# A two-layer hybrid decoder: queries of two expert heads made block by block, half a gate made later, the second block's expert rows written out

## The chip, the cores and the metric

One core of a Trainium2 chip runs the kernel in one launch. The metric is the device time of one execution in microseconds (us). Before the change it is 1875.85 us, the median of three runs (1875.61 to 1876.41).

## The reference

The input is 256 tokens of width 1024, and there are two layers. Each layer has a token mixer (three branches, of which none is touched here, merged by gates and multiplied by an output matrix), a layer norm, and a channel mixer, which is the part that the change is about:

```python
q = (h @ w_q).reshape(B, S, 8, 2, 128)              # 8 heads, two sides each
s1 = einsum('bshd,hnd->bshn', q[..., 0, :], sub_k1)  # 128 scores per side
s2 = einsum('bshd,hnd->bshn', q[..., 1, :], sub_k2)
v1, i1 = top_k(s1, 16); v2, i2 = top_k(s2, 16)       # best 16 of each side
# the best 16 of the 256 sums v1 + v2 name 16 of 128*128 experts
wts = softmax(top_s)
act = gelu(einsum('thkd,td->thk', u_tab[idx], x))    # one dot per expert
out = einsum('thkd->td', act * wts * v_tab[idx])     # weighted sum of rows
ple = sigmoid(h @ ple_gate) * (p @ ple_proj)         # embedding gate, projection
h = layer_norm(alpha * h + out + ple)
```

So every token reads 8 x 16 = 128 expert rows of 2 x 1024 floats (a `u` row and a `v` row, kept side by side, 8 KB), chosen by its own scores.

## The kernel before, in words

The tokens stand in two blocks of 128, one token on each partition. In each layer a dense stage makes the token mixer. Its large products are three fp32r products each (a value split into a high and a low part, lines 760 to 762). Then come the experts, first of block 0, then of block 1.

**A row of experts.** For each of the 128 ranks (8 heads x 16) of a block, GpSimd issues an indirect DMA (line 680 for block 0, line 703 and after it 713 for block 1) that gathers one expert row for each of the 128 tokens, 1 MB, into one of 8 slots. VectorE forms the dot of the `u` half with the tokens (lines 1737, 1767). ScalarE takes gelu, multiplies by the softmax weight and writes a diagonal matrix of the result (lines 1330 to 1334 for block 0, 1354 to 1360 for block 1). TensorE multiplies that diagonal with the `v` half and adds into two PSUM banks `acc` (lines 931, 950). The semaphore `row_used` then frees the slot, and GpSimd may issue the gather of 8 rows later into it. Each fp32 product with 512 columns appears as two records, so that a row is four records of TensorE.

**What else runs beside the rows of block 0.** The order is written out by hand in `steps()`, and all engines follow the same list. Beside a row `("row", r, i)` (number 16r + i) stand steps of TensorE: `wqh` and `wq` (line 791) make the two sides of a head's queries for both blocks at once, 8 products of 256 columns each; `sc` (line 1191) makes a block's 256 scores of a head; `pp` (line 1197) is the embedding's projection; `pgw` (line 823) is a quarter of one half of the embedding gate, for both blocks, four products of 512 columns. Head 0 has its own step per block, `wq0` (line 784), 16 products of 128 columns. Queries of heads 1 and 2 are made ahead of, or in, the first rows; heads 3 to 7 stand beside rows up to 61, `pp` at 62 and 65, the gate from 70 to 106. VectorE picks the 16 best of the head two ahead (`select_head`) in pieces between the dots.

**Block 1** runs in hardware loops: seven turns of a head on GpSimd and TensorE, six on VectorE and ScalarE, with waits against a register and `nop(nofuse=True)` beside them; GpSimd copies eight indices at a time to `stage` (line 695), VectorE copies the scores of a head (line 1552), ScalarE the weights of a head (line 1348). No query, score or gate is left for it.

**Between the blocks** VectorE waits until the last row of block 0 has been added, adds `acc` to block 0's base in two instructions (line 1720) and only then forms block 1's first dot. TensorE waits for that sum, puts block 1's base into `acc` by two products with the identity (line 943) and goes on with the rows.

**The start.** TensorE runs ten products with the identity that nobody reads (`keep_busy`, line 740) before the first transposes of the input (line 836), and ten more after them. Then it makes the pooling branch's input in eight pieces (`poolw`, four quarters of two blocks), with a small product `smallT` between the second and the third quarter, which waits for GpSimd's low part of its weights.

**Weights** come in pieces of 512 KB that SyncE loads through a ring of 7 buffers; some pieces, those of the queries among them, have homes of their own (`EXTRAS`, `extra_home`). A buffer is loaded again once the piece in it has been read (`used`).

Of the kernel before, what the change touches and what calls it, by code (L numbers as in the profile page):

```python
# [25 lines left out]
U32 = mybir.dt.uint32  # L26
ALU = mybir.AluOpType
# [54 lines left out]
SELECT_LINKS = 27  # L82
HALF = TOPK // 2
ROW_LINKS = TOPK


def steps():
# [60 lines left out]
    beside = {(0, 1): [("sc", 0, 2), ("sc", 1, 2)], (0, 6): [("wqh", 1, 1)], (0, 9): [("wq", 1, 1)], (0, 11): [("sc", 0, 3), ("sc", 1, 3)]}  # L148
    halves_at, gate_at = (20, 25, 31, 36, 42, 47, 53, 58), (70, 75, 80, 85, 91, 96, 101, 106)
    beside |= {divmod(n, TOPK): [("wq" if i % 2 else "wqh", 2 + i // 4, i // 2 % 2)] for i, n in enumerate(halves_at)}  # L150
    beside |= {divmod(n + 3, TOPK): [("sc", 0, 4 + i), ("sc", 1, 4 + i)] for i, n in enumerate(halves_at[1::2])}
    beside |= {divmod(62 + 3 * b, TOPK): [("pp", 0, b), ("pp", 1, b)] for b in range(2)}
    beside |= {divmod(n, TOPK): [("pgw", j // 4, j % 4)] for j, n in enumerate(gate_at)}
    beside |= {divmod(gate_at[4 * c + 3] + 1, TOPK): [("pg", c, 0), ("pg", c, 1)] for c in range(2)}
    for r in range(EH):
        for i in range(TOPK):
            s += [("row", r, i)] + beside.get((r, i), [])
    s += [("ln2", 0), ("experts", 1), ("ln2", 1)]
# [3 lines left out]
NO_BANK = {"outa", "wide", "wide_out", "late", "o", "shares", "exps", "softplus", "onorm", "stats", "ln1", "ln2", "select", "texp", "wqh", "pgw", "row", "experts"}  # L162
# [3 lines left out]
def rows_later(kinds, rows):  # L166
# [3 lines left out]
    for step in STEPS[first:]:  # L170
        if step[0] in kinds:
            held.append([rows, step])
            continue
        out.append(step)
        if step[0] == "row":
# [9 lines left out]
def first_products(L):  # L185
# [16 lines left out]
ACT_STEPS = rows_later(("wq", "sc", "pp", "pg"), 1)  # L202
DVE_STEPS = rows_later(("pg",), 2)
FILLS = [s for s in STEPS if s[0] not in NO_BANK]
NBANK = 6


def group_list():
# [20 lines left out]
    for hd in range(EH):  # L229
        if hd:  # L230
            made = ("wq", hd // 2, hd % 2)
            g.append(([made], False, [made, made]))
# [5 lines left out]
    for c in range(2):  # L238
        g.append(([("pg", c, 0), ("pg", c, 1)], False, [None, None, None, ("pg", c, 1)]))
# [7 lines left out]
QUERY_PIECES = [[(GROUP_OF[("wq", hd // 2, hd % 2) if hd else ("wq0", 0)], j) for j in range(2)] for hd in range(EH)]  # L247
KEY_PIECES = [(GROUP_OF["sc", 0, 1], j) for j in range(2)]
PROJECTION_PIECES = [(GROUP_OF["pp", 0, 0], j) for j in range(2)]
EXTRAS = QUERY_PIECES[4] + QUERY_PIECES[5] + PROJECTION_PIECES  # L250
EXTRAS += QUERY_PIECES[3] + QUERY_PIECES[6] + QUERY_PIECES[7] + QUERY_PIECES[1] + QUERY_PIECES[2] + QUERY_PIECES[0] + KEY_PIECES
# [27 lines left out]
def build(nc, x, weights, params, lnrows, consts, experts, cum_rows, out):  # L279
    with ExitStack() as ctx:  # L280
# [88 lines left out]
        stage = sb("stage", 16, U32)  # L369
        upper_lower = sb("upper_lower", 2 * HALVED, U32)  # L370
        wts = sb("wts", NB * RANKS)
        wst, dots, gel, gw = sb("wst", 16), sb("dots", 16), sb("gel", 16), sb("gw", 16)
# [79 lines left out]
        idx_staged, wts_staged = sem("idx_staged"), sem("wts_staged")  # L452
# [47 lines left out]
        def extra_home(L, piece):  # L500
# [6 lines left out]
            if piece in QUERY_PIECES[3]:  # L507
# [83 lines left out]
        def _(sp):  # L591
# [7 lines left out]
            early = QUERY_PIECES[2] + QUERY_PIECES[1] + QUERY_PIECES[3]  # L599
            ahead = {g1 + 2 + 2 * i: early[i:i + 1] for i in range(6)} | {b1 + 8 + 2 * i: QUERY_PIECES[7][i:i + 1] for i in range(2)}  # L600
            ahead |= {o + 2 * i + 1: QUERY_PIECES[6][i:i + 1] for i in range(2)} | {o + 7: QUERY_PIECES[0]}
            ahead |= {o + 10: QUERY_PIECES[4][:1], o + 11: QUERY_PIECES[4][1:], o + 12: QUERY_PIECES[5][:1]}
# [28 lines left out]
        def _(pool):  # L631
# [4 lines left out]
            for L in range(DEPTH):  # L636
                for step in STEPS:
# [45 lines left out]
                    if kind == "experts":  # L683
                        b = step[1]
                        n0 = (L * NB + b) * RANKS

                        def number(r, i):

                            pool.wait_ge(row_used, r * TOPK + (n0 + i + 1))
                            pool.nop(nofuse=True)  # L690
                            if i % HALF == 0:
                                pool.wait_ge(idx_ready, r * 2 + (2 * (L * NB + b) * EH + i // HALF + 1))
                                pool.nop(nofuse=True)
                            if i % RING == 0:
                                nc.gpsimd.tensor_copy(stage[:, i:i + RING], idxu[:, bass.ds(r * TOPK + (b * RANKS + i), RING)]).then_inc(idx_staged, 1)
                                pool.wait_ge(idx_staged, r * 2 + (L * 2 * EH + i // RING + 1))
                                pool.nop(nofuse=True)
                            return bass.IndirectOffsetOnAxis(stage[:, i:i + 1], 0)

                        with pool.Fori(0, EH - 1) as r:  # L700
                            for i in range(TOPK):
                                at_row = number(r, i)
                                nc.gpsimd.indirect_dma_start(slots[i % RING][:, :], None, experts[:, :], at_row).then_inc(slot_in[i % RING], 16)  # L703
                        halves = experts.rearrange("e (s d) -> (e s) d", s=2)
                        for i in range(TOPK):
                            at_row = number(EH - 1, i)
                            if i == RING:
# [1381 lines left out]
```

## Time and profile before

| | |
|---|---|
| median of 3 runs | 1875.85 us |
| the profiled execution: its own time | 1876.75 us |
| its span, first to last instruction | 1874.8 us |
| mean granted clock of TensorE | 0.991 |
| TensorE, VectorE, ScalarE, GpSimd busy | 91%, 73%, 48%, 38% |
| expert gathers (software queue) | 546.57 MB in 75952 packets |
| weights and the like (hardware queue) | 112.74 MB |

Read the shares of busy time as means over two dense stages (about 0 to 289 us and 937 to 1218 us) and two expert stages. The page cuts the span in 40 slices: in the slices of the expert stages the bytes moved per second stand between 410 and 428 GB/s and the DMA engines show full, in the dense stages TensorE shows full and the bytes stand far lower.

### The profile page before, as it was taken

The page shows a single profiled execution, that of the slowest core. Times are in us where ns is not written, and L with a number is a line of the kernel's source. Part 1 is how long each engine was busy: PE and PEld are TensorE (multiplying, and loading weights), DVE is VectorE, ACT ScalarE, POOL GpSimd, SP SyncE. Part 2 cuts the span into 40 slices and gives each one's busy share as a digit, 9 for nine tenths or more (in the row PEclk, how much of TensorE's full clock was granted, in tenths as well). Part 3 has the DMA queues.
Part 4 walks back from the last instruction along what each step waited for, and adds up shares of the span by engine and source line. Part 5 has one row for each costly group of instructions (what it writes and reads, how often), then busy time and mean ns, then how long its engine had stood idle before and what let it go on. Part 6 is the DMA issues. An engine that isn't in the chain of part 4 may idle for free.

```text
span 1874.8 us, 26329 instructions
## 1 busy us (share of the span) xinstructions
PE 1703.7 (91%) x7304; PEld 988.2 (53%) x7304; DVE 1368.8 (73%) x3501; ACT 902.1 (48%) x2245; POOL 704.4 (38%) x593
## 2 busy tenths in 40 slices
PE   9999999999998788787799999999999987878776
PEld 8987886555443232222389778865544432222222
DVE  5887768877677777776569876687777777777755
ACT  5566434444454444445465665345444454444443
POOL 0110003544444555555411100045444554555554
PEclk9999999999999999999999999999999999999999
DMA  6644769999999999999955357799999999999997
GB/s 249 185 128 139 258 230 418 425 427 426 410 427 426 426 427 428 428 428 428 403 182 172 126 167 240 267 426 424 426 424 416 426 427 419 428 427 427 428 421 302
DMA packets 107305, 660.61 MB, mean 352 GB/s; under 512 B 11952, under 2 KB 12352, under 8 KB 41152
## 3 DMA queue, kind: packets, MB, share of 16 engines
q0 software_dynamic: 75952, 546.57, 69.5%
q1 hardware_dynamic: 31248, 112.74, 17.9%
q8 instruction: 53, 0.87, 0.2%
q14 instruction: 52, 0.43, 0.1%
HBM read 658.20 MB, written 1.06 MB: 352 GB/s over the span
## 4 chain that ended last, share of the span: by engine, by line
PE 59%; DMA 19%; issue 9%; ACT 6%; DVE 5%; POOL 1%; DVEq 1%; ACTq 0%; POOLq 0%; SPq 0%
PE acc L931 17%; DMA cst<-experts_dram,stage 8%; PE psum L760 6%; PE psum L762 6%; PE psum L761 6%; DMA arena<-experts_dram,stage 6%; PE psum L791 5%; PE acc L950 5%; DMA arena<-experts_dram,idxu 4%; PE psum L823 1%; PE acc L760 1%; PE psum L850 1%; PE acc L762 1%; PE acc L761 1%; ACT L1354 1%
## 5 line engine op out<-in xcount | busy, mean ns | idle before, releaser
L950 PE MATMUL acc<-arena 128*128 128x512 f32 x896 | 441.3, 621 | 117.9 <-ACT arena L1360 117.8
L931 PE MATMUL acc<-arena 128*128 128x512 f32 x896 | 408.1, 601 | 23.3 <-ACT arena L1334 22.9
L1767 DVE CUSTOM_DVE_ANT_0 arena<-arena,h 128x1024 f32<-128x1024 f32 x224 | 274.7, 1226 | 140.1 <-DMA arena<-experts_dram,stage 60.4
L950 PEld LDWEIGHTS acc<-arena 128*128 128x128 f32 x896 | 157.8, 193 | 399.7 <-issue 399.5
L680 POOL DMA_INDIRECT arena<-experts_dram,idxu x224 | 260.6, 1163 | 280.5 <-PE acc L931 250.6
L1737 DVE CUSTOM_DVE_ANT_0 arena<-arena,h 128x1024 f32<-128x1024 f32 x224 | 274.5, 1225 | 111.8 <-DMA arena<-experts_dram,idxu 105.0
L703 POOL DMA_INDIRECT arena<-experts_dram,stage x196 | 262.9, 1341 | 203.0 <-PE acc L950 159.7
L931 PEld LDWEIGHTS acc<-arena 128*128 128x128 f32 x896 | 166.7, 191 | 238.2 <-issue 168.0
L1614 DVE TENSOR_TENSOR raw_r<-raw,w_hi_r 128x1024 fp32r<-128x1024 f32 x150 | 177.8, 1220 | 62.7 <-ACT w_hi_r L1238 61.6
L1354 ACT ACTIVATE gel<-dots 128x1 f32<-128x1 f32 x256 | 51.9, 203 | 288.8 <-DVE dots L1767 287.4
L1238 ACT ACTIVATE w_hi_r<-raw 128x1024 fp32r<-128x1024 f32 x152 | 154.4, 1054 | 52.5 <-DMA raw<-weights_dram 52.3
L1330 ACT ACTIVATE gel<-dots 128x1 f32<-128x1 f32 x256 | 51.1, 199 | 217.8 <-DVE dots L1737 217.0
L1360 ACT ACTIVATE arena<-cst,gw 128x128 f32<-128x128 f32 x256 | 102.9, 402 | 42.5 <-ACT gw L1357 14.9
L1334 ACT ACTIVATE arena<-cst,gw 128x128 f32<-128x128 f32 x256 | 102.9, 402 | 8.4
L760 PE MATMUL psum<-w_hi_r,hidden_r 128*128 128x512 f32 x256 | 101.4, 396 | 2.3 <-POOL raw_r L727 1.9
L762 PE MATMUL psum<-w_hi_r,hidden_r 128*128 128x512 f32 x256 | 100.3, 392 | 0.0
L761 PE MATMUL psum<-raw_r,hidden_r 128*128 128x512 f32 x256 | 100.0, 391 | 0.0
L760 PE MATMUL psum<-hidden_r,w_hi_r 128*128 128x256 f32 x320 | 91.4, 286 | 0.0
L761 PE MATMUL psum<-hidden_r,w_hi_r 128*128 128x256 f32 x320 | 90.5, 283 | 0.0
L762 PE MATMUL psum<-hidden_r,raw_r 128*128 128x256 f32 x320 | 90.5, 283 | 0.0
L1357 ACT ACTIVATE gw<-gel,wst 128x1 f32<-128x1 f32 x256 | 75.4, 295 | 24.0 <-ACT gel L1354 0.5
L669 POOL DMA_DIRECT2D lnr<-lnrows_dram x2 | 1.1, 536 | 221.0 <-DVE h L1607 221.0
(306 smaller groups left out, 2764.9 us busy)
## 6 DMA issues: line engine op xcount, KB each, us to landing
raw<-weights_dram SPq DMA_DIRECT2D x168, 512.0 KB, 3.7
arena<-weights_dram SPq DMA_DIRECT2D x20, 512.0 KB, 4.9
w_hi<-weights_dram SPq DMA_DIRECT2D x12, 512.0 KB, 6.6
lnr<-lnrows_dram POOLq DMA_DIRECT2D x4, 1024.0 KB, 6.6
arena<-experts_dram,idxu POOLq DMA_INDIRECT x224, 11.8
arena<-experts_dram,stage POOLq DMA_INDIRECT x222, 13.9
lnr<-cum_dram POOLq DMA_DIRECT2D x2, 1024.0 KB, 9.0
cst<-weights_dram SPq DMA_DIRECT2D x4, 512.0 KB, 5.2
```

The lines of the kernel that those rows point to most:

```text
L680: nc.gpsimd.indirect_dma_start(slots[n % RING][:, :], None, experts[:, :], bass.IndirectOffsetOnAxis(idxu[:, n:n + 1], 0)).then_inc(slot_i ...
L703: nc.gpsimd.indirect_dma_start(slots[i % RING][:, :], None, experts[:, :], at_row).then_inc(slot_in[i % RING], 16)
L760: mm(dst, left[0], right[0], start=start, stop=False)
L761: mm(dst, left[0], right[1], start=False, stop=False)
L762: return mm(dst, left[1], right[0], start=False, stop=stop)
L931: last = mm(acc[:, c * 512:(c + 1) * 512], diag[:, i % 4, :], slots[n % RING][:, D + c * 512:D + (c + 1) * 512], start=n == 0, stop=n == R ...
L950: last = mm(acc[:, c * 512:(c + 1) * 512], diag[:, i % 4, :], slots[i % RING][:, D + c * 512:D + (c + 1) * 512], start=False, stop=ends)
L1238: AC(w_hi[:, n % HIS, :], raw[:, raw_slot(L, piece), :], ACT.Copy).then_inc(w_hi_ready, 1)
L1334: AC(diag[:, i % 4, :], ident, ACT.Copy, scale=gw[:, i:i + 1]).then_inc(diag_ready, 1)
L1614: TT(w_lo[:, s, :], raw[:, s, :], w_hi[:, n % HIS, :].bitcast(F32), ALU.subtract).then_inc(w_lo_ready, 1)
L1737: nc.vector.tensor_tensor_reduce(slot[:, 0:D], slot[:, 0:D], h[:, 0, :], 1.0, 0.0, ALU.mult, ALU.add, dots[:, i:i + 1]).then_inc(dot_ready, 1)
L1767: nc.vector.tensor_tensor_reduce(slots[i % RING][:, 0:D], slots[i % RING][:, 0:D], h[:, b, :], 1.0, 0.0, ALU.mult, ALU.add, dots[:, i:i + ...
```

## The change

Eight edits, in the order of the kernel:

- The queries of heads 3 and 5 are made by block (`qbh`, `qb`: one side each, 8 products of 128 columns). Block 0's stand beside rows 6, 9 and 28, 31; block 1's of head 3 beside rows 110, 114; block 1's of head 5 beside rows 24, 28 of block 1. Heads 4, 6, 7 stay together.
- The embedding gate is made per block. Its first half stands at rows 70 to 87, block 0's second half at rows 90 to 99, block 1's second half at rows 38, 46, 54, 66 of block 1. A gate piece's ring buffer is now released when the whole half is done.
- Block 1's rows are written out as steps `row1`, without loops, copies of indices, weights and scores, or `nop`s.
- VectorE's sum of block 0 (`ln2`, 0) comes after block 1's first dot.
- Block 1's base is added to `acc` at its row 80 instead of before its first row.
- VectorE waits for the scores of block 1 head by head instead of for all at once.
- `keep_busy` runs 5 and 4 products instead of 10 and 10; in the first layer `smallT` moves one quarter later.
- Query pieces 3 and 4 change homes.

```diff
-    beside = {(0, 1): [("sc", 0, 2), ("sc", 1, 2)], (0, 6): [("wqh", 1, 1)], (0, 9): [("wq", 1, 1)], (0, 11): [("sc", 0, 3), ("sc", 1, 3)]}
-    halves_at, gate_at = (20, 25, 31, 36, 42, 47, 53, 58), (70, 75, 80, 85, 91, 96, 101, 106)
...
+    first[1] = [("sc", b, 2) for b in range(NB)]
+    apart(first, 0, 3, (6, 9, 12))
+    together(4, (16, 21, 24))
+    apart(first, 0, 5, (28, 31, 34))
+    together(6, (38, 43, 46))
+    together(7, (50, 55, 58))
+    for b in range(NB):
+        first[62 + 4 * b] = [("pp", c, b) for c in range(2)]
+    gated_embedding(first, 0, range(NB), (70, 72, 75, 77, 80, 82, 85, 87))
+    gated_embedding(first, 1, (0,), (90, 93, 96, 99))
+    apart(first, 1, 3, (110, 114, 117))
+    apart(second, 1, 5, (24, 28, 31))
+    gated_embedding(second, 1, (1,), (38, 46, 54, 66))
+    for n in range(RANKS):
+        s += [("row", *divmod(n, TOPK))] + first.get(n, [])
+    s += [("ln2", 0), ("experts", 1)]
+    for n in range(RANKS):
+        s += [("row1", *divmod(n, TOPK))] + second.get(n, [])
...
-            first += products(0, (j,)) + products(1, (j,)) + [("smallT",)] * (j == 1)
+            first += products(0, (j,)) + products(1, (j,)) + [("smallT",)] * (j == 2)
...
+DVE_STEPS.remove(("ln2", 0))
+DVE_STEPS.insert(DVE_STEPS.index(("row1", 0, 0)) + 1, ("ln2", 0))
...
-        g.append(([("pg", c, 0), ("pg", c, 1)], False, [None, None, None, ("pg", c, 1)]))
+        g.append(([("pg", c, 0), ("pg", c, 1)], False, [("pg", c, 1)] * 4))
...
+            def query_side(L, b, hd, ps, i):
+
+                w = whole(L, *QUERY_PIECES[hd][i])
+                for k in range(KT):
+                    last = mm(ps[:, i * P:(i + 1) * P], w[:, k * P:(k + 1) * P], h1w[:, k, b * P:(b + 1) * P], start=k == 0, stop=k == KT - 1)
+                return last
...
-            keep_busy(10)
+            keep_busy(5)
...
-                            keep_busy(10)
+                            keep_busy(4)
...
-                        pe.wait_ge(base_ready, L * NB + 2)
-                        for c in range(2):
-                            mm(acc[:, c * 512:(c + 1) * 512], ident, base[:, 1, c * 512:(c + 1) * 512], start=True, stop=False)
...
+                    if kind == "row1":
+                        _, r, i = step
+                        n = r * TOPK + i
+                        n0 = (L * NB + 1) * RANKS
+                        if n == BASE_AT:
+                            pe.wait_ge(base_ready, L * NB + 2)
+                            for c in range(2):
+                                mm(acc[:, c * 512:(c + 1) * 512], ident, base[:, 1, c * 512:(c + 1) * 512], start=False, stop=False)
...
+                        pe.wait_ge(diag_ready, n0 + n + 2)
...
+            def weight(L, b, r, i):
+
+                n = b * RANKS + r * TOPK + i
+                made = L * NB * RANKS + n
+                if i == 0:
+                    act.wait_ge(wts_ready, (L * NB + b) * EH + r + 1)
+                act.wait_ge(dot_ready, made + 1)
+                AC(gel[:, i:i + 1], dots[:, i:i + 1], ACT.Gelu).then_inc(dot_used, 1)
+                act.wait_ge(dot_used, made + 1 + TOPK)
+                link(AC(gw[:, i:i + 1], gel[:, i:i + 1], ACT.Copy, scale=wts[:, n:n + 1]))
+                act.wait_ge(row_used, made + RING - 3)
+                AC(diag[:, i % 4, :], ident, ACT.Copy, scale=gw[:, i:i + 1]).then_inc(diag_ready, 1)
...
-                        with dve.Fori(0, turns) as r:
-                            head(r, "select", True)
...
+                        if i == 0 and r < EH - AHEAD:
+                            choose = select_head(L, EH + r + AHEAD)
+                            dve.wait_ge(*drained(L, ("sc", 1, r + AHEAD)))
+                        elif i == 0 and r == EH - AHEAD:
+                            choose = itertools.chain(statistics(base[:, 0, :]), norm(base[:, 0, :], base[:, 0, :], 0, L * 4 + 3, h2_ready))
+                        dve.wait_ge(dot_used, L * NB * RANKS + n + 1)
+                        dve.wait_ge(*landed(L, n))
```

## Rows read from the trace of the kernel before

**Rows 1.** Busy time by stretch: length, engines' busy us, clock, DMA share, GB/s

```profile
core 0: us, PE busy (x) PEld busy (x) DVE busy (x) ACT busy (x) POOL busy (x), PEclk, DMA share, GB/s
470.00:490.00 20.00, 20.00 (x48) 8.67 (x47) 14.62 (x49) 8.73 (x29) 8.80 (x8) 1.00 0.97 389
640.00:870.00 230.00, 182.85 (x374) 66.45 (x374) 171.77 (x496) 104.70 (x308) 131.31 (x106) 0.98 1.01 427
1400.00:1430.00 30.00, 30.00 (x71) 13.22 (x70) 20.15 (x61) 15.12 (x44) 12.68 (x13) 1.00 1.00 407
1560.00:1570.00 10.00, 9.36 (x21) 3.30 (x20) 8.18 (x22) 4.62 (x16) 4.70 (x6) 1.00 0.99 392
1790.00:1810.00 20.00, 15.38 (x35) 5.91 (x33) 12.02 (x20) 9.72 (x27) 11.76 (x10) 1.00 1.01 412
```

**Rows 2.** The chain that ended last, layer 0's rows: start, us, what

```profile
281.76 3.81 PE psum L784 x32
382.67 3.45 PE psum L791 x16
482.42 3.43 PE psum L823 x8
485.86 8.58 PE acc L931 x20
```

**Rows 3.** Timeline, scores and a late gather: start, us, instruction, [idle before <-releaser]

```profile
286.09 0.68 PE L1191 MATMUL psum<-raw,arena 128*128 128x128 f32 x4 [0.52 <-issue]
475.74 1.83 POOL L680 DMA_INDIRECT arena<-experts_dram,idxu  x1 [4.19 <-PE acc L931]
```

**Rows 4.** Timeline between the blocks, layer 1

```profile
1551.35 1.28 DVE L1720 TENSOR_TENSOR arena<-arena,acc 128x512 f32<-128x512 f32 x2 [3.13 <-issue]
1552.69 1.98 PE L943 MATMUL acc<-arena,cst 128*128 128x512 f32 x4 [1.43 <-DVE arena L1720]
1555.74 1.95 PE L950 MATMUL acc<-arena 128*128 128x512 f32 x4 [1.06 <-ACT arena L1360]
1558.05 0.19 POOL L695 COPY stage<-idxu 128x8 uint32 x1 [4.99 <-PE acc L950]
```

**Rows 5.** Timeline, ScalarE's diagonal in block 0 and in block 1

```profile
1548.82 0.40 ACT L1334 ACTIVATE arena<-cst,gw 128x128 f32<-128x128 f32 x1
1562.42 0.40 ACT L1360 ACTIVATE arena<-cst,gw 128x128 f32<-128x128 f32 x1 [0.21 <-ACT gw L1357]
```

**Rows 6.** Timeline, the first 18 us

```profile
1.18 0.42 SPq L594 DMA_DIRECT2D h<-x_dram  x1
2.77 4.08 PE L740 MATMUL acc<-cst 128*128 128x128 f32 x20 [2.77 <-DMA cst<-consts_dram]
6.58 0.91 PEld L836 LDWEIGHTS psum<-cst,h 128*128 128x128 f32 x8
8.90 2.40 PE L740 MATMUL acc<-cst 128*128 128x128 f32 x20
11.06 0.47 PE L760 MATMUL psum<-w_hi_r,hidden_r 128*128 128x512 f32 x1
17.82 0.29 PE L760 MATMUL psum<-hidden_r,w_small 128*16 128x256 f32 x1 [1.05 <-POOL w_small L641]
```

**Rows 7.** Line 594, the input's two loads, issue to landing

```profile
DMA to landing us min/median/max: 4.3/5.0/5.8
```

**Rows 8.** Lines 1737 and 1767, VectorE's idle before its dots by releaser: us, times

```profile
  DMA arena<-experts_dram,idxu: 105.0, 143
...
  issue: 71.1, 62
```

**Rows 9.** The page's first line and its queues of instruction code: packets, MB

```profile
span 1874.8 us, 26329 instructions
...
q8 instruction: 53, 0.87, 0.2%
q14 instruction: 52, 0.43, 0.1%
```

More of the change, by code:

```diff
@@ L152, in steps, with apart @@
[L152 to L158, printed above, removed]
+    first, second = {}, {}
+    def apart(beside, b, hd, rows):
+        for kind, n in zip(("qbh", "qb", "sc"), rows):
+            beside[n] = [(kind, b, hd)]
@@ new lines, in together, with gated_embedding @@
+    def together(hd, rows):
+        for kind, n in zip(("wqh", "wq"), rows):
+            first[n] = [(kind, hd // 2, hd % 2)]
+        first[rows[2]] = [("sc", b, hd) for b in range(NB)]
+    def gated_embedding(beside, c, blocks, rows):
+        for n, (j, b) in zip(rows, itertools.product(range(4), blocks)):
+            beside[n] = [("pgw", c, j, b)]
+            if (j, b) == (3, blocks[-1]):
+                beside[n + 1] = [("pg", c, b) for b in blocks]
+    first[1] = [("sc", b, 2) for b in range(NB)]
@@ L174, in rows_later @@
         out.append(step)
-        if step[0] == "row":
+        if step[0] in ("row", "row1"):
             for wait in held:
@@ L230, in group_list @@
         if hd:
-            made = ("wq", hd // 2, hd % 2)
-            g.append(([made], False, [made, made]))
+            made = [query(b, hd) for b in range(NB if hd in APART else 1)]
+            g.append((made, False, [made[-1], made[-1]]))
         else:
@@ L506, in extra_home @@
                 return hidden[:, KT * T + j * PIECE:][:, 0:PIECE]
[L507 removed]
+            if piece in QUERY_PIECES[4]:
                 return scs_flat[:, (2 * j + 1) * PIECE:][:, 0:PIECE]
@@ L815, in gate_piece, with embedding_piece @@
                     read(L, g, j, ends[b])
-            def embedding_piece(L, g, j, blocks):
+            def embedding_piece(L, g, j, ps, b):
                 w = whole(L, g, j)
-                for ps, b in blocks:
-                    for i in range(2):
-                        k = 2 * j + i
-                        ends[b] = mm(ps, h1w[:, k, b * P:(b + 1) * P], w[:, i * 512:(i + 1) * 512], start=k == 0, stop=k == KT - 1)
-                read(L, g, j, ends[1])
+                for i in range(2):
+                    k = 2 * j + i
+                    last = mm(ps, h1w[:, k, b * P:(b + 1) * P], w[:, i * 512:(i + 1) * 512], start=k == 0, stop=k == KT - 1)
+                return last
             def turn(L, b, q):
@@ L967, in _ @@
+                    if kind in ("qbh", "qb"):
+                        _, b, hd = step
+                        bk, use = place(L, query(b, hd))
+                        if kind == "qbh":
+                            pe.wait_ge(bank_drained[bk], use)
+                        last = query_side(L, b, hd, psum[:, bk, :], int(kind == "qb"))
+                        if kind == "qb":
+                            last.then_inc(bank_filled[bk], 1)
                         continue
@@ new lines, in _ @@
+                    if kind == "row1":
+                        _, r, i = step
+                        weight(L, 1, r, i)
+                        if i == 12 and r < EH - AHEAD:
+                            shifted_exp(L, EH + r + AHEAD)
+                        if (r, i) == (EH - 2, 2):
+                            roots()
+                            act.wait_ge(var_ready, L * 4 + 3)
+                            inv_sqrt(rstd[:, :], mv[:, 1:2], mv[:, 1:2], rstd_ready)
+                        if (r, i) == (EH - 1, 5) and L + 1 < DEPTH:
+                            for q in range(2):
+                                columns_hi(L + 1, 0, q)
@@ new lines, in _ @@
+                        continue
+                    if kind == "row1":
+                        _, r, i = step
+                        n = RANKS + r * TOPK + i
+                        if i == 0 and r < EH - AHEAD:
[5 more added lines that the diff above has]
+                        dve.wait_ge(*landed(L, n))
+                        slot = slots[n % RING]
+                        nc.vector.tensor_tensor_reduce(slot[:, 0:D], slot[:, 0:D], h[:, 1, :], 1.0, 0.0, ALU.mult, ALU.add, dots[:, i:i + 1]).then_inc(dot_ready, 1)
+                        next(choose, None)
+                        if (r, i) == (EH - 1, 5) and L + 1 < DEPTH:
+                            for q in range(2):
+                                columns_lo(L + 1, 0, q)
+                        if i == TOPK - 1:
```

286 lines of the change are left out of this document (93 added, 193 removed).

## The prediction, made before the changed kernel was run

> **What bounds the kernel now.** I read part 2 of the page first (its slices tell dense stages from expert stages), then the busy time by stretch, then the chain of waits, then timelines where a stretch falls short. In the expert stages the bound is the gather itself: 128 rows of 8 KB are 1.049 MB, and at the 427 GB/s that the steady stretch 640 to 870 us holds [rows 1] one row takes 1.049 MB / 427 GB/s = 2.46 us. TensorE needs less: five rows in 8.58 us, 1.72 us a row [rows 2]. So a row leaves TensorE 0.74 us, a block 128 x 0.74 = 94.7 us, and whatever is written beside block 0's rows has to fit in that. Where it fits, an edit of it is worth nothing; time is lost only where fewer bytes move than 427 GB/s. The reader is to see four such stretches in [rows 1]: 470 to 490 at 389, 1400 to 1430 at 407, 1560 to 1570 at 392, 1790 to 1810 at 412. The dense stages are bound by TensorE, and the change touches only the first 18 us of them.
>
> **1. The two holes in the middle of block 0.** Lost: 20 us x (427 - 389)/427 = 1.78 us in layer 0, 30 x (427 - 407)/427 = 1.41 us in layer 1; 3.2 us. In both TensorE is busy throughout, and a gather stands 4.19 us waiting for a row's products [rows 1, 3]: the queue runs dry because TensorE is behind. Its load before row 70: heads 3 to 7 are 10 sides at 3.45 us = 34.5; scores of heads 2 to 7, 12 x about 0.6 = 7.2 (0.68 for the four records in [rows 3]); projection 2 x 3.43 = 6.9 (priced as the equal gate piece of [rows 2]); together 48.6 us against 70 x 0.74 = 51.8 us, in lumps. That is full, and the hole stands right behind it. After: heads 3 and 5 of block 0 cost 3.81 us each (head 0's price for one block, [rows 2]), heads 4, 6, 7 still 6.9 each, scores 10 x 0.6, projection 6.9: 7.6 + 20.7 + 6.0 + 6.9 = 41.2 us, 7.4 us less. From row 70 on the gate was 8 x 3.43 = 27.4 us in 37 rows, which have 27.4 us to spare: no recovery before row 107. It becomes 12 x 1.72 = 20.6 us in 30 rows (22 us), with head 3's 4.4 us after row 109. Block 0 carries 48.6 + 27.4 = 76.0 us before and 41.2 + 20.6 + 4.4 = 66.2 after, of 94.7. I take the whole 3.2 us; bounds 0 (the queue runs dry for another reason) and 3.2 (the rest already moves at full rate). What moves to block 1 is 3.81 + 0.6 + 4 x 1.72 = 11.3 us, which is hidden: TensorE is busy 183 of 230 us there and the gathers stay at 427 [rows 1]. The DMAs that move with it are the gate's last piece, loaded when the first half is done (row 87, needed at row 99: 12 rows, 29 us), and the pieces of heads 3 and 4, which exchange homes and go on the same queue in the same number.
>
> **2. Between the blocks.** In layer 1 VectorE's sum starts at 1551.35 after 3.13 us idle, the base's products at 1552.69, the first row of block 1 only at 1555.74, and GpSimd's next index copy, which that row frees, at 1558.05 [rows 4]. With the first dot ahead of the sum and no base product, that row can start at about 1552.7, 3.0 us earlier, and its gather follows without a copy. The hole behind it is 10 x (427 - 392)/427 = 0.82 us [rows 1]; I take 0.8, bounds 0 and 0.8. The added wait puts VectorE's second dot and the first step of a head's selection behind the sum, where the second dot stood already. The base's 1.98 us come back at row 80, in slack.
>
> **3. Loops written out.** VectorE's idle before block 1's dots counts 71.1 us of issue, that before block 0's is the DMA [rows 8]. That is hidden by the gathers except where rows run out: 20 x (427 - 412)/427 = 0.70 us at 1790 to 1810, where loops end [rows 1], of which I take half, 0.35 (bounds 0 and 0.7: layer norm and table loads stand there too and stay); and the last rows of each layer, where ScalarE loses 0.21 us before a diagonal in block 1 and none in block 0 [rows 5]: 2 x 0.2 = 0.4, of which I take 0.3 (bounds 0 and 0.4, since layer 0's end meets the next weights). Against it stands the code. It comes through the same DMA, 0.87 + 0.43 = 1.30 MB for 26329 executed instructions [rows 9], at least 49 bytes each. The stretch of 230 us executes 374 + 374 + 496 + 308 + 106 = 1658 instructions that count [rows 1], block 1's 314 us some 2260, of which five sixths are repeats now: 3800 in two layers, with waits perhaps 4800, at 50 to 60 bytes 0.2 to 0.3 MB. At 427 GB/s an estimate of 0.7 us lost, bounds 0 and 1.4 (twice the code).
>
> By the Trainium skill (Runtime: NRT & Kernel Launch, Instruction fetch mechanics) a taken branch to code outside the window that is held forces a fetch before the engine goes on. By it the whole 0.70 us would go, and the sum would be 0.35 us better; that the loops' turns at 640 to 870 us move 427 GB/s shows no such price while rows are in stock.
>
> **4. The start.** The 20 records of the first ten idle products take 4.08 us from 2.77, and the transposes start at 6.58 [rows 6], although the input's first load is there at 1.18 + 4.3 = 5.5 (with 5.8 it would be 7.0, after they began) [rows 6, 7]: up to 1.1 us. The second batch takes 2.40 us from 8.90 and ends where the first real product starts, 11.06; with 4 products it takes 0.96. Chain by chain the first real product can start about 1.0 us earlier, at 10.0. `smallT` then waits 1.05 us for its weights at 17.82 [rows 6]; one quarter later, behind another 2.7 us of products, it does not. Together 2.1 us at most, and TensorE, which bounds the dense stage, carries it on. The risk is the clock: the first batch ran at the half level (4.08 us against 2.40 for the same work, [rows 6]) and TensorE was busy without a break until it rose; now it stands idle from about 4.8 to 5.5 and again before 8. If it rises only after the real products have begun, they lose what the first batch lost, 4.08 - 2.40 = 1.7 us, and the transposes some tenths: bounds -0.3 and 2.1. I take 1.3, above the middle, because five products and the transposes still go ahead.
>
> By the Trainium skill (TensorE: Matmul & The Clock Gate, the part on the warm-up) the throttled clock is the default and only sustained activity releases it. By that page taking idle products out speaks against the change: the second rival below. The trace agrees in so far as the first batch is the slow one.
>
> **Sum.** 3.2 + 0.8 + 0.35 + 0.3 - 0.7 + 1.3 = 5.25 us off the profiled execution's 1876.75 (span 1874.8), 1871.5. That execution is 0.9 above the median 1875.85, so the median to expect is 1870.6. About 0.2%, 3.75 us, is what a measurement of this kernel can tell from no change: the line is 1872.1.
>
> **The rivals.**
>
> *The holes stay* (rather, others take their place): the queue runs dry because of bursts on VectorE or ScalarE, and the new lumps make new ones. For it: a second gate half alone adds a table load and a sigmoid per layer, and the sums of part 1 are near the limit, not over it. Against it: TensorE is named as the releaser, and it is busy 20 of 20 and 30 of 30 us in the two stretches. Then 3.2 and 0.35 stay: 1874.1.
>
> *The clock comes late at the start*: part 4 gives -0.3 to 0.4 instead of 1.3, about 1.3 us less: 1871.9 to 1872.3, on the line.
>
> *Written-out code arrives late*: the 0.3 MB are 18 packets as long as those of the larger code queue (0.87 MB / 53 = 16.4 KB), and each comes behind the gathers in the queue. If an engine waits for it and the slots run dry, each costs; from 5.25/18 = 0.3 us a packet the gain is gone, at 0.5 us it is slower by 0.2%, at 1 us the time is 1888. Against it: block 0 is written out already under the same load, and issue is not what its dots wait for [rows 8].
>
> **Chances.** The forecast 0.57, with a range of its own of 1868.5 to 1872; late clock 0.20, holes 0.14, late code 0.06; 0.03 for better than 1868. Faster by over 0.2% is the forecast nearly whole, 0.03, and under a third of the late clock: 0.65; within 0.2% 0.29, slower 0.06. The range takes in the clock and the holes: 1867 to 1875.
>
> **What would show it.** Part 1: no stretch under 420 GB/s between rows 60 and 110 of either block 0. Part 2: the first row of block 1 within 2 us of the sum's start, no base product before it. Part 3: a few hundred KB more in the two code queues, no issue idle before block 1's dots, the same 427 GB/s. Part 4: the first real product near 10.0, no wait before the small one, its records as long as the 0.47 us of [rows 6] and not twice that. The prediction is wrong if the expert stages lose time anywhere at 427 GB/s, if a new stretch under 420 appears in block 1, or if the first dense stage ends no earlier.

## The result, and the profile after

The changed kernel takes 1879.61 us (median of 20 runs, 1877.78 to 1881.05) against 1875.72 us before (20 runs, 1874.54 to 1877.18): ratio 1.0018, 95% interval 1.0012 to 1.0025. It is slower by 2.2 to 4.7 us; forecast were 1870.6 and a gain. The profiled execution took 1879.71 us, with a granted clock of 0.996.

The first things to read are the page's first line and its two queues of instruction code (packets, MB); they answer to [rows 9]. The changed kernel executes 3162 instructions fewer and loads 17 packets of code more:

```profile
span 1877.9 us, 23167 instructions
...
q8 instruction: 59, 0.97, 0.2%
q14 instruction: 63, 0.51, 0.1%
```

Next the busy time by stretch, with the columns of [rows 1]. The stretches that fell short before now move 425 to 428 GB/s: all four holes are closed. The steady stretch of block 1 has fallen from 427 to 422, with a new hole inside it:

```profile
470.00:490.00 20.00, 20.00 (x48) 8.75 (x47) 14.94 (x48) 8.84 (x29) 7.81 (x8) 1.00 1.01 425
640.00:870.00 230.00, 189.08 (x422) 72.15 (x420) 167.38 (x491) 106.18 (x303) 102.39 (x92) 0.99 1.01 422
780.00:810.00 30.00, 25.95 (x54) 9.98 (x53) 23.41 (x75) 13.95 (x39) 12.65 (x12) 0.94 1.00 398
1400.00:1430.00 30.00, 30.00 (x71) 13.12 (x70) 21.31 (x64) 14.43 (x41) 12.67 (x13) 1.00 1.01 426
1560.00:1570.00 10.00, 8.09 (x18) 2.71 (x16) 6.69 (x19) 3.74 (x14) 3.74 (x4) 1.00 1.01 428
1790.00:1810.00 20.00, 16.59 (x33) 6.25 (x32) 12.50 (x20) 9.71 (x27) 9.90 (x9) 0.91 1.01 426
```

Bytes per second do not tell when a row is complete. The dots do, since each waits for its row. Below, counting a layer's rows 0 to 255, are the dots of rows 144 and 240 of layer 0, first before, then after (start, us, instruction): 235.41 us before, 240.50 us after for the same 96 rows of block 1.

```profile
660.37 1.23 DVE L1767 CUSTOM_DVE_ANT_0 arena<-arena,h 128x1024 f32<-128x1024 f32 x1 [1.22 <-DMA arena<-experts_dram,stage]
895.78 1.23 DVE L1767 CUSTOM_DVE_ANT_0 arena<-arena,h 128x1024 f32<-128x1024 f32 x1 [1.20 <-issue]
```

```profile
658.54 1.23 DVE L1760 CUSTOM_DVE_ANT_0 arena<-arena,h 128x1024 f32<-128x1024 f32 x1 [1.18 <-DMA arena<-experts_dram,idxu]
899.04 1.22 DVE L1760 CUSTOM_DVE_ANT_0 arena<-arena,h 128x1024 f32<-128x1024 f32 x1 [1.19 <-DMA arena<-experts_dram,idxu]
```

The 5.1 us come in single steps. In the changed kernel the dots stand 2.44 us apart, and 3.4 us at rows 150, 170, 189, 210 and 234. One such step in the timeline, rows 149 to 152: the third line comes 3.42 us after the second, and VectorE waited 1.88 us for the gather. It is the landings that have moved, not VectorE: the trace has the gathers of rows 149 to 151 land at 670.69, 674.11 and 676.55 us, each 0.13 to 0.16 us before its dot, although that of row 150 was issued in good time (15.3 us before it landed; row 149's 13.6). The landings stand 3.4 us apart in the same way at the other four steps.

```profile
670.85 1.23 DVE L1760 CUSTOM_DVE_ANT_0 arena<-arena,h 128x1024 f32<-128x1024 f32 x1 [0.75 <-DMA arena<-experts_dram,idxu]
672.00 0.08 DVE L1760 DVE_READ_ACCUMULATOR2_ANT dots<- 128x1 f32 x1
...
674.27 1.22 DVE L1760 CUSTOM_DVE_ANT_0 arena<-arena,h 128x1024 f32<-128x1024 f32 x1 [1.88 <-DMA arena<-experts_dram,idxu]
...
676.68 1.22 DVE L1760 CUSTOM_DVE_ANT_0 cst<-cst,h 128x1024 f32<-128x1024 f32 x1 [0.68 <-DMA cst<-experts_dram,idxu]
```

The DMA queues in the 3 us of that step, 671.5 to 674.5 (packets, MB, share of 16 engines' time), show one packet of code; and the stretch by busy time shows that the 16 DMA engines together lost nothing meanwhile (426 GB/s, last column):

```profile
q0 software_dynamic: 172, 1.26, 100.7%
q14 instruction: 1, 0.01, 0.6%
...
671.00:677.00 6.00, 4.06 (x9) 1.35 (x8) 3.41 (x8) 1.80 (x6) 2.21 (x3) 1.00 1.01 426
```

VectorE's idle before its dots answers to [rows 8]: line 1760 (block 1) no longer shows any issue, and the DMA is named for all but 0.8 us.

```profile
  DMA arena<-experts_dram,idxu: 160.2, 183
  DMA cst<-experts_dram,idxu: 29.1, 28
  DVE tiu L1535: 0.6, 4
  DVE arena L1547: 0.2, 1
```

### The profile page after: what moved, and what is told of

The parts are those of the page before. It is cut to its first block, busy times and chain, and to the rows that moved or that the text cites. A ratio compares the mean times of both kernels' runs of the same rounds, so it can differ in the third digit from the quotient of the medians.

```text
span 1877.9 us, 23167 instructions
## 1 busy us (share of the span) xinstructions
PE 1704.0 (91%) x7410; PEld 987.9 (53%) x7410; DVE 1360.8 (72%) x3489; ACT 908.3 (48%) x2239; POOL 610.2 (32%) x561
## 4 chain that ended last, share of the span: by engine, by line
PE 38%; DMA 33%; issue 15%; DVE 6%; ACT 6%; POOL 2%; DVEq 0%; SPq 0%; POOLq 0%; ACTq 0%
DMA arena<-experts_dram,idxu 28%; PE acc L955 11%; PE acc L979 6%; DMA cst<-experts_dram,idxu 4%; PE psum L778 3%; PE psum L779 3%; PE psum L780 3%; DVE arena L1736 2%; PE psum L816 2%; ACT arena L1249 2%; DVE arena L1760 2%; PE psum L847 1%; PE acc L778 1%; ACT L1245 1%; PE acc L780 1%
## 5 line engine op out<-in xcount | busy, mean ns | idle before, releaser
L728 POOL DMA_INDIRECT arena<-experts_dram,idxu x222 | 246.0, 1108 | 318.2 <-PE acc L979 284.9
L713 POOL DMA_INDIRECT arena<-experts_dram,idxu x224 | 248.4, 1109 | 283.6 <-PE acc L955 253.8
L1247 ACT ACTIVATE gw<-gel,wts 128x1 f32<-128x1 f32 x512 | 150.8, 295 | 16.6
L979 PE MATMUL acc<-cst,arena 128*128 128x512 f32 x128 | 62.2, 609 | 6.5 <-ACT arena L1249 6.0
L955 PE MATMUL acc<-cst,arena 128*128 128x512 f32 x128 | 61.0, 598 | 1.3 <-ACT arena L1249 1.3
## 6 DMA issues: line engine op xcount, KB each, us to landing
arena<-experts_dram,idxu POOLq DMA_INDIRECT x446, 14.5
```

The lines of the kernel that those rows point to most:

```text
L713: nc.gpsimd.indirect_dma_start(slots[n % RING][:, :], None, experts[:, :], bass.IndirectOffsetOnAxis(idxu[:, n:n + 1], 0)).then_inc(slot_i ...
L728: nc.gpsimd.indirect_dma_start(slots[n % RING][:, :], None, experts[:, :], bass.IndirectOffsetOnAxis(idxu[:, n:n + 1], 0)).then_inc(slot_i ...
L955: last = mm(acc[:, c * 512:(c + 1) * 512], diag[:, i % 4, :], slots[n % RING][:, D + c * 512:D + (c + 1) * 512], start=n == 0, stop=n == R ...
L979: last = mm(acc[:, c * 512:(c + 1) * 512], diag[:, i % 4, :], slots[n % RING][:, D + c * 512:D + (c + 1) * 512], start=n == 0, stop=n == R ...
```

## Experiments

Behind each time stands the ratio to the kernel before, measured again on the same chip, with its 95% interval. Steps are spacings of 3.3 to 3.6 us between dots in rows 144 to 240 of layer 0.

**Which part of the change costs.** Theory at this point: code, and GpSimd's above all, because the steps come every 20 rows and GpSimd's rows are the most regular. Rivals: any engine's code, or the work moved into block 1.

```diff
 # e1: the changed kernel, GpSimd's loop of before put back
-    for n in range(RANKS, NB * RANKS): ... indirect_dma_start(..., idxu[:, n:n + 1])
+    with pool.Fori(0, EH - 1) as r: ... indirect_dma_start(..., stage[:, i:i + 1])
 # e2: the kernel before, GpSimd's loop written out (the reverse)
 # e3: the changed kernel, work of block 1 back in block 0
-    gated_embedding(first, 1, (0,), (90, 93, 96, 99))
-    apart(first, 1, 3, (110, 114, 117))
-    apart(second, 1, 5, (24, 28, 31))
-    gated_embedding(second, 1, (1,), (38, 46, 54, 66))
+    gated_embedding(first, 1, range(NB), (90, 92, 94, 96, 98, 100, 102, 104))
+    apart(first, 1, 3, (108, 112, 115))
+    apart(first, 1, 5, (118, 122, 125))
 # e4: the kernel before, the new opening alone
-    keep_busy(10)   (twice)              [("smallT",)] * (j == 1)
+    keep_busy(5), keep_busy(4)           [("smallT",)] * (j == 2)
```

> The changed kernel with GpSimd alone back in its loop over the rows of block 1; the other engines stay written out, the moved work stays where the change put it. Theory G (GpSimd's own written-out code: each refill of it, about every 20 rows, stops the gathers for 1.0 us): the five 3.4 us steps per layer between the dots of block 1 go, 2 x 5 x 1.0 us off 1879.6, so 1869 to 1871. Theory A (any engine's code costs, each packet about 0.55 us): GpSimd's share of the added packets is about five of nine per layer, so 1873.5 to 1875, and some steps stay. Theory W (the work moved into block 1): 1879 to 1880, the steps stay.

> The kernel before with GpSimd alone written out in block 1; all else as before, loops on the other engines. G: steps of 3.4 us every 20 rows of block 1 as in the changed kernel, five per layer, and the index copies and the turn at the loop's end saved: 1884 to 1886 against 1875.7. A: about five packets per layer at 0.55 us: 1880 to 1881.5. W: 1875 to 1876.

> The changed kernel with head 5's query and scores and the second gate half of block 1 put back beside block 0's rows (gate pieces at rows 90 to 104, head 3 at 108 to 115, head 5 at 118 to 125); block 1 has rows only, written out on all engines. W: the losses of block 1 (3.2 us in layer 0, 2.4 in layer 1, counted from row 128) go: 1873 to 1875. G and A: 1879 to 1881, the five steps per layer stay.

> The kernel before with the change's opening alone (five and four idle products, the small product one quarter later). By the first gather of the changed kernel, 288.32 us against 289.26: 0.9 us faster, 1874.8. Were the opening worth the 1.3 of the forecast: 1874.4; were it nothing: 1875.7.

e1: 1880.44 us, 1.0022 (1.0013 to 1.0031); the five steps stay. e2: 1877.05, 1.0002 (0.9993 to 1.0011); no step. GpSimd's code is not it: my theory fell on both. (e2 loads one packet of q14 more than the kernel before, 53 against 52, so it shows that GpSimd's code is little, not what a packet of it would cost.) e3: 1880.03, 1.0017 (1.0008 to 1.0026), five steps: the moved work is not it either. e4: 1875.89, 0.9998 (0.9989 to 1.0007), which leaves room for 2.1 us gained and for 1.3 lost, and so settles nothing between 0 and 1.3.

**Which engine.** Loops of the kernel before were written out one engine at a time, nothing else changed.

```diff
 # e5: TensorE                          # e6: ScalarE        # e7: VectorE
-    with pe.Fori(0, EH - 1) as r:        act.Fori(0, turns)   dve.Fori(0, turns)
+    for r in range(EH - 1):              for r in range(turns): head(r, "select", False)
 # and the loop's nop(nofuse=True) taken out; e8: all four engines
```

> The kernel before with TensorE's loop over block 1 alone written out (its schedule, opening and boundary as before). The traces of block 1 written out show three series of code packets: one of q14 every 20 rows, each with a 3.4 us step between dots, one of q14 every 30 rows and one of q8 every 29 rows, both without a step. Theory O (the code of one of TensorE, ScalarE and VectorE makes the steps; which one is open): the one engine gives five steps per layer, 1884 to 1886 against 1875.7; the two others 1875 to 1876.5. Theory A (every packet costs alike): each of the three about a third of the loss, some 3 us: 1878 to 1879.5 in each.

> The kernel before with ScalarE's loop over block 1 alone written out. O: 1884 to 1886 with five 3.4 us steps per layer if ScalarE's code makes them, 1875 to 1876.5 without steps if not. A: 1878 to 1879.5.

> The kernel before with VectorE's loop over block 1 alone written out. O: 1884 to 1886 with five 3.4 us steps per layer if VectorE's code makes them, 1875 to 1876.5 without steps if not. A: 1878 to 1879.5.

> The kernel before with all four loops of block 1 written out, and no other part of the change (no moved work, no new opening, the sum of block 0 still ahead of the first dot). A and O: the steps of the changed kernel, five per layer, and without the gains of opening and boundary (0.9 + about 2.5 us by the dots): 1882 to 1885. If the steps need more than the written code (the boundary's new order, the moved work): 1875 to 1877.

e5: 1875.75, 0.9999 (0.999 to 1.0008). e6: 1874.70, 0.9993 (0.9984 to 1.0002). Neither has a step. e7: 1883.65, 1.0042 (1.0028 to 1.0055), five steps. e8: 1882.17, 1.0033 (1.002 to 1.0045), five steps. So it is VectorE's code alone. The price is not one of packets as such: ScalarE's written-out rows bring packets of the same queue, five of q14 between 640 and 870 us where [rows 1] had the same gathers (two before), and the dots stay on 2.44. Three of them come at rows 167, 196 and 226; the changed kernel's three packets of q14 without a step come at rows 167, 197 and 226, so these are ScalarE's and the five with a step VectorE's.

**Back to a loop, and more code.** e9 puts VectorE's loop back into the changed kernel, e10 also gives block 0 one, which the kernel before never had. e11 and e12 were to add code by empty instructions.

```diff
 # e9: rows 16 to 95 of block 1      # e10: and rows 16 to 79 of block 0
-    for row1 1..5 of VectorE written out
+    with dve.Fori(0, 5) as t: choose = select_head(L, t + (EH + 1 + AHEAD), t); 16 dots
+    with dve.Fori(0, 4) as t: ...   (waits for a count `scored` that ScalarE keeps)
 # e11 (VectorE), e12 (ScalarE): beside each row of block 1
+    for _ in range(6): engine.nop(nofuse=True)
```

> The changed kernel with VectorE alone back in a loop over heads 1 to 5 of block 1 (rows 16 to 95; head 0 and the last two heads stay written out); for that head 5's steps go to rows 5, 9 and 12 and the base's product to row 104. Theory V (each refill of VectorE's own code holds up the gathers for 1.0 us, no other engine's does): the steps between row 150 and row 234 go, four or five of 1.0 us per layer, and what the rest of the change gained stays: 1870 to 1872, about the forecast. Rival: the rest of the change gains nothing, and the boundary's gain is lost again elsewhere: 1875 to 1877.

> As the run before, and VectorE's heads 1 to 4 of block 0 (rows 16 to 79) as a loop too, which the kernel before did not have; ScalarE counts the scores that the loop waits for. V: block 0's steps near 428 and 480 us and one more go in both layers, less a refill where the loop ends: 2 to 3 us per layer below the run before, 1864 to 1868. Rival (block 0 is bound by TensorE, a step there costs nothing at the end): equal to the run before within 1 us.

> The changed kernel with six empty instructions after each dot of block 1 on VectorE, 768 per layer; nothing else. At the 8.2 KB of a packet in 20 rows VectorE has some 410 bytes a row; if an empty instruction is about as long as another, its code is nearly doubled. V: about twice as many steps, four or five more per layer: 1887 to 1890. Rival (the steps are VectorE's busy time or its waits, not its code): the empty instructions fit into its 0.7 us of idle time a row: 1879 to 1881.

> The changed kernel with six empty instructions per row of block 1 on ScalarE instead, 768 per layer: several more packets of the same 8.2 KB queue. V (VectorE's packets alone cost): 1879 to 1881. A (each packet costs): 1882 to 1886.

e9: 1874.80, 0.9995 (0.9986 to 1.0004): 4.8 us below the changed kernel, between the two expectations. Rows 144 to 240 take 237.32 us, 3.2 less than in the changed kernel and 1.9 more than with the old loop; one step is left at row 158 and a shorter one (3.22 us) at row 147, each behind a packet, both in the loop's first turn; the later turns have none. e10: 1871.76, 0.9978 (0.9969 to 0.9987), faster than both kernels, though by less than expected; rows 32 to 127 of block 0 take 236.72 us against 237.77. e11 (1879.66) and e12 (1879.66) say nothing: both execute the same 23167 instructions as the changed kernel and load a packet less, so the empty instructions were never in the code.

**Dose, another engine's code, and the best version.**

```diff
 # e13: the changed kernel, VectorE, after each dot of block 1
+    for k in range(6): nc.vector.memset(pad[:, 6 * (n % 32) + k:][:, 0:1], 0.0)
 # e14: the kernel before, SyncE, at rows 8 to 103 of block 1
+    sp.wait_ge(row_used, ...)
+    for _ in range(12): sp.sem_inc(more, 1)
 # e15: e10 with block 1's loop turned by a row; head 5 beside block 0 as in e3
+    dot(row 0); sum of block 0
+    with dve.Fori(0, 6) as t: rows 16t + 1 to 16t + 16
```

> The changed kernel with six more instructions per row of block 1 on VectorE (each clears one unused element per partition, some 0.06 to 0.1 us), 768 per layer. Theory V (each refill of VectorE's code holds the gathers up for 1.0 us): packets of VectorE's queue in block 1 about double, four to six more 1.0 us steps per layer: 1887 to 1892. Rival (the step is no matter of code, but of VectorE's waits): the 0.4 to 0.6 us a row fit into its idle 0.7: 1879 to 1881.

> The kernel before with SyncE, idle there, waiting for each of rows 8 to 103 of block 1 and then executing twelve semaphore increments that nobody waits for: 1152 instructions and 96 waits per layer, code that comes through the same DMA engines. Theory V (only VectorE's packets lie in the way): 1875 to 1877 and no new steps. Theory M (the DMA engine with the most packets is the late one, whichever engine they are for): if SyncE's packets outnumber the five per block that VectorE has, the steps appear at its packets, 3 to 8 us per layer: 1882 to 1890.

> The changed kernel with VectorE in loops over rows 16 to 79 of block 0 and over rows 1 to 96 of block 1, the loop's body turned by one row so that the first dot still precedes the sum and no head is written out at the start of block 1; head 5 is back beside block 0. V: one refill per layer less than with head 0 written out, some 1 to 2 us below that kernel's 1871.8: 1870 to 1871. Rival (the steps left in block 1 are the loops' own entry and exit): 1871.5 to 1872.5.

e13: 1894.11, 1.0098 (1.0083 to 1.0114), 14.5 us above the changed kernel and more than expected; nine steps in rows 144 to 240 of layer 0, eleven in those of layer 1 (two of these, at rows 486 and 487, stand where block 0's result is written). In its timeline the six clears take 0.10 us in all, so VectorE's time is no cause; the dot behind still waits 1.69 us for a gather:

```profile
700.35 1.23 DVE L1761 CUSTOM_DVE_ANT_0 arena<-arena,h 128x1024 f32<-128x1024 f32 x1 [1.16 <-DMA arena<-experts_dram,idxu]
701.50 0.08 DVE L1761 DVE_READ_ACCUMULATOR2_ANT dots<- 128x1 f32 x1
701.53 0.10 DVE L1763 MEMSET pad<- 128x1 f32 x6
...
703.76 1.22 DVE L1761 CUSTOM_DVE_ANT_0 arena<-arena,h 128x1024 f32<-128x1024 f32 x1 [1.69 <-DMA arena<-experts_dram,idxu]
```

e14: 1876.51, 1.0001 (0.9992 to 1.001), no step in rows 144 to 240. In layer 1 two stand at 1813 and 1816 us, but not for code: SyncE, held up by its added waits, sends block 0's result only then, at 1807.90 us instead of 1797.29, and that write's packets lie between 1811.4 and 1815.5. In the kernel before the same write lies between 1801.2 and 1805.7, and rows 486 and 487 are the long ones (3.10 and 3.39 us).

```profile
1807.90 0.35 SPq L633 DMA_DIRECT2D out_dram<-h  x1
```

Of SyncE's eighteen packets in rows 144 to 240 of both layers three are followed by 0.4 to 0.7 us against the kernel before (rows 233, 468, 479); by the last row of block 1, 0.0 us of it is left in layer 0 and 0.6 in layer 1. So SyncE's code is not wholly free, but far from 1.0 us a packet. The queues between 640 and 870 us, first of e13, then of e14 with the stretch by busy time under each: thirteen and ten packets of the same queue, one kernel 11 GB/s short, the other not at all.

```profile
q14 instruction: 13, 0.11, 0.1%
q8 instruction: 4, 0.07, 0.1%
...
640.00:870.00 230.00, 185.67 (x418) 70.91 (x417) 171.07 (x1025) 101.40 (x293) 96.34 (x91) 1.00 1.01 416
```

```profile
q14 instruction: 10, 0.08, 0.1%
q8 instruction: 1, 0.02, 0.0%
...
640.00:870.00 230.00, 179.19 (x374) 64.42 (x374) 171.72 (x497) 104.60 (x308) 130.66 (x105) 1.00 1.01 427
```

So it matters whose code a packet holds; the queue and the number of packets do not explain it. e15: 1870.25, 0.997 (0.9958 to 0.9982): the fastest version, 9.4 us below the changed kernel, with 427 GB/s throughout 640 to 870 us:

```profile
640.00:870.00 230.00, 185.35 (x390) 68.16 (x389) 172.49 (x500) 107.21 (x307) 96.22 (x94) 1.00 1.01 427
```

All runs on one scale, the time between the dots of two rows in us, worked out from the timelines:

```
rows of layer 0 / 1           144-240   steps   400-496   VectorE in block 1
before, e2, e4, e5, e6      235.40-.41    0   236.65-237.05  loop
e14 (SyncE's code)            235.84      0     238.69       loop
changed                       240.50      5     241.58       written out
e1, e3                     240.41-241.53  5   241.39-.62     written out
e7, e8                     239.99-240.09  5   240.53-241.01  written out
e13                           244.49      9     246.87       written out, longer
e9                            237.32      1     238.49       loop from row 16
e10                           236.32      0     238.54       loop from row 16
e15                           236.37      1     237.59       loop from row 1
```

(Rows of layer 1 count on, 256 to 511; they are 144 to 240 of that layer. A time without steps can hold a part of one. In layer 1 every kernel loses some 1 to 2 us at rows 486 and 487, e14 at 490 and 491, beside the write of block 0's result. e15 has a second long spacing, 3.80 us at row 225, where VectorE leaves its loop; there the row had landed 1.5 us before.)

## Why the prediction was wrong, step by step

**Code (part 3): the step that failed.** I added up the new code as bytes, 0.2 to 0.3 MB, and spread them over 427 GB/s, that is over all 16 DMA engines: 0.7 us. The amount was about right (0.97 + 0.51 against 0.87 + 0.43 MB, 0.18 MB more). The price was not: writing out the four loops costs 6.1 us by the medians of e8 (3.8 to 8.4 by its interval), gains at the loops' ends and between the blocks included, where I had reckoned 0.65 gained and 0.7 lost. (The gains are there: 426 GB/s at 1790 to 1810, and no wait before ScalarE's diagonal, [rows 5].)

```profile
1552.62 0.40 ACT L1249 ACTIVATE arena<-cst,gw 128x128 f32<-128x128 f32 x1
```

What was mis-sized is VectorE's share: five steps in 96 rows, 1.0 us each, (240.50 - 235.41)/5. One of the five is not new, it has moved: rows 240 to 255 take 34.35 us in either layer where they took 35.33, since the kernel before has a step of its own there, where its VectorE is written out as well (its loop makes six of the eight heads):

```profile
904.09 1.22 DVE L1767 CUSTOM_DVE_ANT_0 arena<-arena,h 128x1024 f32<-128x1024 f32 x1 [2.19 <-issue]
```

The name issue is the profile's here: the gather of this row, 243, landed 3.4 us after the one before it and 0.12 us before the dot. So the 71.1 us of issue in [rows 8] are in part waits for gathers, and that line 1760 names the DMA instead is in part a change of name.

The packets of the other engines cost nothing that these runs resolve. Two of the forecast's own signs of being wrong were there: the expert stages lose time at 426 GB/s, and a stretch of block 1 stands under 420.

The rival "written-out code arrives late" was the case, at a chance of 0.06, and in a form that I did not have: only one engine's packets count, and they hold up the gathers rather than the engine. I turned it down because block 0 was written out already and its dots do not wait for issue [rows 8]. They wait for DMA there, and that was the sign: in the trace of before block 0 has the steps, of 3.4 us at 426.5 and 479.0 us for instance, each behind a packet of q14; I looked at its bytes and not at its dots. The sum over rows would have been a poorer sign. Block 0's rows 32 to 127 take 237.83 us, 2.503 us a row, block 1's rows 144 to 240 235.41, 2.452 us: 4.9 us over 96 rows, close to the 5.1 that writing out block 1 then cost, but by chance, since VectorE's loop over rows 16 to 79 of block 0 took back only 1.1 us (e10) and 0.8 us (e15); most of the 4.9 is other work beside these rows.

By the Trainium skill (Runtime: NRT & Kernel Launch, Instruction fetch mechanics) crossing into the next block of code costs one queue bump that is mostly hidden, and kernels prefer full unrolling where possible. For TensorE, ScalarE and SyncE these runs agree (e5, e6, e14: intervals from 0.16% faster to 0.1% slower); for GpSimd, with one packet more, e2 can tell little. For VectorE beside saturated gathers they differ: 1.0 us a packet. The measurement decides.

**Holes in block 0 (part 1): closed, and worth nothing.** The bytes came as forecast: 425 and 426 GB/s where there were 389 and 407. The wait that I had named as the cause did not go with them: a gather still stands 4.08 us for a row's products, as one did 4.19 [rows 3]:

```profile
473.94 0.94 POOL L713 DMA_INDIRECT arena<-experts_dram,idxu  x1 [4.08 <-PE acc L955]
475.75 0.94 POOL L713 DMA_INDIRECT arena<-experts_dram,idxu  x1 [0.87 <-PE acc L955]
```

And rows 32 to 127 take 237.77 us instead of 237.83, and rows 256 to 383 318.63 instead of 318.67. I had taken a stretch below 427 GB/s for lost time. A reading that fits, but that no view shows: a row is complete when its last part lands, so one DMA engine that is behind delays the rows, and the mean over 16 engines falls only later, where those that are ahead have run out of rows. The new hole at 780 to 810 would be of that kind. At the step of 671 to 677 the mean is 426, and e8, with the same five steps, moves 426 at 780 to 810: hole and loss do not go together.

**Between the blocks (part 2): 2.0 us, over the upper bound of 0.8, its cause not separated.** The sum starts behind the first dot, TensorE's first row 1.3 us after it, with no product of the base between (answers to [rows 4], layer 1):

```profile
1550.73 1.23 DVE L1760 CUSTOM_DVE_ANT_0 arena<-arena,h 128x1024 f32<-128x1024 f32 x1 [1.59 <-DMA arena<-experts_dram,idxu]
...
1552.40 1.28 DVE L1719 TENSOR_TENSOR arena<-arena,acc 128x512 f32<-128x512 f32 x2
...
1553.74 1.98 PE L979 MATMUL acc<-arena 128*128 128x512 f32 x4 [1.56 <-DVE arena L1719]
```

Rows 127 to 144 take 42.64 us instead of 43.53, rows 383 to 400 42.61 instead of 43.73, 2.0 us together. e7, where the sum still comes first but VectorE is written out, has 42.57 and 42.78; e15, with loop and first dot ahead, 42.57 and 42.56. Either of the two gives it, and they do not add.

**The start (part 4): another way, and less.** The first real product starts at 11.32, not at the forecast 10.0 and not before the old 11.06 [rows 6]: the records of the half pace last longer, as the second rival had it. Ten of the first idle batch take 2.50 us and the second batch's eight 1.67, 0.21 to 0.25 us each, where the second batch of before took 0.12 [rows 6]; the real products have 0.48 us and less from the first. (The clock column of the stretches reads 1.00 from 2 us on in both kernels; the pace is read from the records.) What was gained fits the small product, which waited 1.05 us [rows 6] and now starts at 19.61 without a wait.

```profile
2.72 2.50 PE L758 MATMUL acc<-cst 128*128 128x128 f32 x10 [2.72 <-DMA cst<-consts_dram]
5.66 1.97 PE L860 MATMUL psum<-cst,h 128*128 128x128 f32 x8 [0.44 <-DMA h<-x_dram]
8.13 1.97 PE L860 MATMUL psum<-cst,h 128*128 128x128 f32 x8 [0.50 <-DMA h<-x_dram]
9.89 1.67 PE L758 MATMUL acc<-cst 128*128 128x128 f32 x8
11.32 0.48 PE L778 MATMUL psum<-w_hi_r,hidden_r 128*128 128x512 f32 x1
...
19.61 0.28 PE L778 MATMUL psum<-hidden_r,w_small 128*16 128x256 f32 x1
```

The first dot stands 0.94 us earlier than before in this pair of profiles; over the seven profiles with the old opening and the ten with the new one the means differ by 1.0, but they scatter by 1.2 and 2.5. e4 alone found 0.3 (2.1 gained to 1.3 lost).

**The sum**, by the dots of the two traces: 9.6 us lost in rows 144 to 240 of both layers (5.1 and 4.5), 2.0 back in rows 240 to 255, 2.0 between the blocks, 0.9 at the start, and 1.6 in all the rest, 1.3 of it between the layers (where other runs lie between 1.3 gained and 0.6 lost): 3.1 us slower, as the spans have it (1877.9 against 1874.8); the medians say 3.9. By the medians of e8, whose 6.1 us hold the gain between the blocks already, and 0.3 to 1.0 off at the start it would be 5.1 to 5.8, with e8's interval 2.8 to 8.1: too wide to tell more. e15 came out at 1870.25, by the forecast's number, for a reason that the forecast did not have: VectorE back in loops, in block 0 as well. That is luck, not a forecast.

## What to carry to other kernels

Where a transfer stream is the bound, look at when its pieces arrive and not at its bytes per second: a hole in the mean may cost nothing and a full mean may hide a late engine. Compare a written-out stretch and a looped one of the same trace per row before taking a loop away, and take loops away one engine at a time. Code is priced by whose it is: here 8 KB of VectorE's cost 1.0 us, while nearly twice as many such packets for SyncE left the time as it was.

## What the runs showed of the hardware that was not expected

- A packet of the q14 queue is 8.1 KB (0.51 MB / 63). One for VectorE beside gathers at 427 GB/s comes with a delay of 1.0 us in their landing: all 14 steps in rows 144 to 240 of layer 0 of the changed kernel and e13 stand 1.8 to 2.5 us behind the start of such a packet, and at each the gather lands 3.4 us after the one before it, VectorE's dot 0.13 to 0.16 us behind. The packet itself takes 0.31 us in the trace, so it is not its own time that is lost.
- Packets of the same queue for ScalarE and SyncE mostly do not come with one (e6, e14). Why VectorE's do stays open; that they travel on the DMA engine that finishes last would explain it, but no view shows single DMA engines, and it was not tried.
- `nop(nofuse=True)` without a wait beside it left the count of executed instructions unchanged (23167 in e11 and e12): it is no means of lengthening code.
